# One raw bias table per near head, masked by GpSimd instead of VectorE, in a two-layer attention and expert kernel

## The reference, cut to what matters

```python
def one_row(r):
    r0 = jnp.clip(r - wr // 2, 0, rows - wr)             # rows = wr = 8: r0 is 0
    k_nb = ...[:, :, :, col_idx]                          # 16 columns around each query column
    bias = jnp.take(rpb_cols, r0 + jnp.arange(wr) - r + (NA_ROWS - 1), axis=1)
    s_loc = einsum(q_r, k_nb) * scale + transpose(bias)
    s_ctx = einsum(q_r, k_ctx) * scale
    p = softmax(concatenate([s_loc, s_ctx]))
```

## Time and profile before

| | us |
|---|---|
| median of 3 runs (3445.88 to 3447.69) | 3447.33 |
| the profiled execution | 3442.6 |
| its span in the profile | 3440.5 |
| end of the input projection, first mask load | 259.4 |
| first near scores | 327.4 |
| first product of the output projection | 487.9 |
| first U loads issued | 535.7 |

### The profile page before, as it was taken

The page is one execution under the profiler, slowest core; times in us unless marked ns, Lnnn a source line. Parts: engine busy times, 40 slices in busy tenths (PEclk is TensorE's granted clock), DMA queues, the critical chain, the costliest instruction groups (busy, mean ns, idle before and its releaser), DMA issues.

```text
span 3440.5 us, 45632 instructions
## 1 busy us (share of the span) xinstructions
PE 3297.2 (96%) x17004; PEld 2879.3 (84%) x17004; DVE 2183.3 (63%) x4167; ACT 1083.2 (31%) x1491; POOL 1837.6 (53%) x1166
## 2 busy tenths in 40 slices
PE   7998379999999999999999999999999999999999
PEld 3886257888878888999999778888888888999998
DVE  7877342488745422899998341688555323999997
ACT  3226244233334322222222333233334322222222
POOL 0000014347788861877772463357888752777761
PEclk9999689999999999999999999999999999999999
DMA  7772521146988894999998122255669865999995
GB/s 283 265 258 57 191 80 71 49 141 155 244 229 167 173 251 148 366 361 357 384 359 301 62 74 86 89 142 143 144 147 177 181 164 206 370 362 360 359 361 214
DMA packets 569952, 733.82 MB, mean 213 GB/s; under 512 B 272130, under 2 KB 404867, under 8 KB 553092
## 3 DMA queue, kind: packets, MB, share of 16 engines
q1 hardware_dynamic: 414084, 529.10, 47.5%
q0 software_dynamic: 118784, 134.68, 15.2%
q10 hardware_dynamic: 36864, 67.13, 5.4%
HBM read 610.92 MB, written 119.80 MB: 212 GB/s over the span
## 4 chain that ended last, share of the span: by engine, by line
PE 89%; SPq 5%; DVE 3%; DMA 1%; issue 1%; ACT 1%; DVEq 0%; ACTq 0%
PE ps L1508 41%; PE ps L1553 30%; PE ps L1468 5%; PE ps L1417 4%; PE ps L1280 4%; SPq L746 3%; SPq L728 1%; PE ps L1528 1%; PE ps L1458 1%; DVE macc L1793 1%; DMA modall<-in_w_mod 0%; DVE xm L1772 0%; PE ps L1232 0%; PE ps L1406 0%; SPq L739 0%
## 5 line engine op out<-in xcount | busy, mean ns | idle before, releaser
L1642 POOL DMA_INDIRECT G_scratch<-pick,gidx x512 | 887.0, 1732 | 283.1 <-issue 211.1
L1508 PE MATMUL ps<-xhi,Uhi 128*128 128x512 f32 x2048 | 801.0, 391 | 2.4 <-DVE Ulo L1992 2.4
L1508 PE MATMUL ps<-xhi,Ulo 128*128 128x512 f32 x2048 | 797.7, 390 | 0.0
L1508 PE MATMUL ps<-xlo,Uhi 128*128 128x512 f32 x2048 | 797.1, 389 | 0.0
L1553 PE MATMUL ps<-Hhi,Vhi 128*128 128x384 f32 x2048 | 686.0, 335 | 3.7 <-DVE Hlo L2202 3.7
L1553 PE MATMUL ps<-Hlo,Vhi 128*128 128x384 f32 x2048 | 684.7, 334 | 0.0
L1553 PE MATMUL ps<-Hhi,Vlo 128*128 128x384 f32 x2048 | 684.7, 334 | 0.0
L1992 DVE TENSOR_TENSOR Ulo<-Uraw,Uhi 128x1024 fp32r<-128x1024 f32 x230 | 281.8, 1226 | 578.9 <-ACT Uhi L1070 577.5
L1133 ACT CAST Vhi<-Vraw 128x1024 fp32r<-128x1024 f32 x256 | 269.9, 1054 | 779.6 <-PE ps L1553 764.6
L1649 POOL DMA_INDIRECT picked<-act_scratch,aidx x256 | 381.5, 1490 | 229.6 <-DMA act_scratch<-act_st 152.2
L1508 PEld LDWEIGHTS ps<-xhi,Uhi 128*128 128x128 f32 x2048 | 384.7, 188 | 81.3 <-DVE Ulo L1992 2.9
(11 more groups left out here) (297 smaller groups left out, 3979.2 us busy)
## 6 DMA issues: line engine op xcount, KB each, us to landing
Uraw<-in_UT SPq DMA_DIRECT2D x128, 1024.0 KB
Vraw<-in_V SPq DMA_DIRECT2D x256, 512.0 KB, 5.5
act_scratch<-act_st ACTq DMA_DIRECT2D x256, 256.0 KB
act<-act_scratch SPq DMA_DIRECT2D x256, 192.0 KB, 5.6
modw<-in_w_mod SPq DMA_DIRECT2D x80, 512.0 KB, 4.7
G_scratch<-zeros SPq DMA_DIRECT2D x32, 1024.0 KB, 10.2
Gin<-G_scratch SPq DMA_DIRECT2D x256, 128.0 KB
ring<-in_query SPq DMA_DIRECT2D x8, 2048.0 KB, 8.0
```

What stands on the lines that cost most here:

```text
L1508: mm = nc.tensor.matmul(up_bank(m), w, x[:, k, :], start=(k == 0 and j == 0), stop=(k == KT - 1 and j == 2))
L1642: nc.gpsimd.indirect_dma_start(G_dram[layer].rearrange("m p (t o) -> (m p t) o", o=1), bass.IndirectOffsetOnAxis(ap=gidx[r][:, h * TOPK + ...
```

## The change

There are five edits.

1. `braw` holds only the 8 to 40 band (256 elements a map). SyncE issues 16 loads a head, 64 in all. The three bands' tables are parts of this one, since the bias depends on the distance alone; `TABLE_PARTS` says which columns of it go where.
2. The mask comes in three DMAs, whose source is repeated over the 8 rows with a step of zero.
3. The 16 zero stores go out after the last query weight of the first four, ahead of the loads of U.
4. `masked_bias(h)` is GpSimd's, before `mix_rest`: wait for the loads; scale the raw table; for h of 2 and 3 wait until the exps of the last unit that reads the table buffer are done; ten additions. VectorE waits for `bias_masked` at the first maxima of each near head (`qt == 0`).
5. `xm` of n = 0: the reads are dense (`(r c) -> r c`) and the write goes through `(c r) -> r c`, with a step of 8 elements (32 bytes).

```diff
-TABLE_PARTS = (((0, 0, 24, 0), (1, 8, 32, 0)), ((1, 0, 8, 24), (2, 8, 24, 0), (2, 0, 8, 16)))
+TABLE_PARTS = (((0, 8, 32, 0), (1, 8, 32, 0)), ((1, 0, 8, 24), (2, 8, 24, 0), (2, 0, 8, 16)))
-        braw = [sb(f"braw{n}", at, [P, 2, TABLE_AT[-1]]) for n, at in enumerate((45, 168.5))]
+        braw = [sb(f"braw{n}", at, [P, 2, NEAR_W[1]]) for n, at in enumerate((45, 168.5))]
...
                     for n, j in enumerate(TABLE_BANDS):
-                        for r in range(NA_ROWS):
-                            sp.dma_start(mask[r:P:NA_ROWS, MASK_AT[n]:MASK_AT[n + 1]],
-                                         a["mask"][j * BAND:(j + 1) * BAND, BANDS[j][0]:BANDS[j][1]]
-                                         ).then_inc(bias_in[0], 16)
+                        c0, c1 = BANDS[j]
+                        sp.dma_start(mask[:, MASK_AT[n]:MASK_AT[n + 1]],
+                                     a["mask"][j * BAND:(j + 1) * BAND, c0:c1].unsqueeze(1).to_broadcast(
+                                         [BAND, NA_ROWS, c1 - c0])).then_inc(bias_in[0], 16)
                 for r in range(NA_ROWS):
-                    for n, j in enumerate(TABLE_BANDS):
-                        c0, c1 = BANDS[j]
-                        for m in range(2):
-                            sp.dma_start(
-                                braw[h % 2][r:P:NA_ROWS, m, TABLE_AT[n]:TABLE_AT[n + 1]].rearrange(
-                                    "q (s k) -> q s k", s=NA_ROWS),
-                                a["btab"][2 * h + m, j * BAND:(j + 1) * BAND,
-                                          NA_ROWS - 1 - r:2 * NA_ROWS - 1 - r, c0:c1]).then_inc(bias_in[h % 2], 16)
-                if h == 1:
-                    sp.wait_ge(zeros_ready, 1)
-                    for n in range(NZERO):
-                        zero_gates(0, n)
+                    for m in range(2):
+                        sp.dma_start(
+                            braw[h % 2][r:P:NA_ROWS, m, :].rearrange("q (s k) -> q s k", s=NA_ROWS),
+                            a["btab"][2 * h + m, BAND:2 * BAND, NA_ROWS - 1 - r:2 * NA_ROWS - 1 - r,
+                                      BANDS[1][0]:BANDS[1][1]]).then_inc(bias_in[h % 2], 16)
...
             load_chunk(W_Q0)
             load_chunk(W_Q0 + 1)
+            sp.wait_ge(zeros_ready, 1)
+            for n in range(NZERO):
+                zero_gates(0, n)
...
+            def masked_bias(h):
+                pool.wait_ge(bias_in[h % 2], 16 * (2 * NA_ROWS * (h // 2 + 1) + (0 if h % 2 else len(TABLE_BANDS))))
+                if h == 0:
+                    pool.wait_ge(proj_out, sum(e[0] == "copy" for e in in_evict) + 4)
+                    nc.gpsimd.tensor_scalar(mask[:, :], mask[:, :], 1.0 / QK_SCALE, None, ALU.mult)
+                nc.gpsimd.tensor_scalar(braw[h % 2][:, :, :], braw[h % 2][:, :, :], 1.0 / QK_SCALE, None, ALU.mult
+                                        ).then_inc(proj_out, 1)
+                pool.wait_ge(proj_out, sum(e[0] == "copy" for e in in_evict) + 5 + h)
+                if h >= 2:
+                    pool.wait_ge(exp_done, 2 * (HEAD_END + TT * (h - 1)))
+                for m in range(2):
+                    for n, c0, c1, to in TABLE_PARTS[0] + TABLE_PARTS[1]:
+                        rows = slice(TABLE_AT[n], TABLE_AT[n + 1])
+                        first = MASK_AT[n] + c0 - (8 if n == 0 else 0)
+                        last = nc.gpsimd.tensor_tensor(
+                            by_column(btab[h % 2][:, m, rows])[:, to:to + c1 - c0, :],
+                            by_row(braw[h % 2][:, m, :])[:, c0:c1, :],
+                            mask[:, first:first + c1 - c0].unsqueeze(2).to_broadcast([P, c1 - c0, NA_ROWS]), ALU.add)
+                last.then_inc(bias_masked, 1)
...
+            for h in range(HB // 2):
+                masked_bias(h)
             mix_rest(0, 2 * KT)
...
                     if n == 0:
-                        to, rows, roots_of = by_column(to), by_row(rows), by_row(inv)
+                        to = to.rearrange("p (c r) -> p r c", r=NA_ROWS)
+                        rows, roots_of = (x.rearrange("p (r c) -> p r c", r=NA_ROWS) for x in (rows, inv))
...
+                    if qt == 0:
+                        dve.wait_ge(bias_masked, h + 1)
...
                     maxima(u + 2)
-                    ahead = u + 2 + TT - HEAD_END
-                    if 0 <= ahead < TT * (HB // 2):
-                        masked_bias(ahead // TT, ahead % TT)
```

## The result

The changed kernel takes 3356.14 us (median of 4 runs, 3353.45 to 3358.24) beside 3446.61 for the kernel before (4 runs, 3445.07 to 3447.69): ratio 0.9737, 95% interval 0.9721 to 0.9754. It is faster by 90.5 us, and the forecast of 3362.4 (own range 3353 to 3371) was 6.3 too high. The sum was made against the profiled execution and is best judged there: forecast 3357.7, measured 3357.07, with a span of 3355.2 against 3440.5.

What follows compares the result with a forecast made beforehand. Bound in the near stretch: the number of DMA issues and one big transfer ahead of small ones, not bytes. 73.7 + 9.6 + 0.9 + 3.7 - 2.0 - 3.0 + 2.0 = 84.9 us off 3447.3 gives 3362.4, range 3353 to 3371.

Steps and rivals of the forecast that it cites:

- The stands: VectorE's three waits for table loads before making masked bias tables all go: 73.7 us gained.
- Masking off VectorE: Near units: twelve masking parts leave VectorE, each worth 0.8 of a 1.0 us difference between units: 9.6 us gained.
- GpSimd's sharing: VectorE operations beside GpSimd's new work lose time on the shared port pair, some 14 hits of 0.2 us: -3.0 us.
- Cold TensorE: Slow-clock transposes, products and scores behind the three stands go: 1.8 us a stand, two thirds counted, 3.7 us gained.
- the table change: ScalarE's function table change for the square root, formerly inside the 53 us stand, is uncovered before exps(20): -2.0 us.
- Diff units: Four masking parts in the last diff units leave VectorE, a quarter of them counted: 0.9 us gained.
- Zeros: The 16 zero stores, moved behind the second query weight on SyncE's queue, cost nothing; U loads keep 50 us to spare.
- Strided writes: Input scalings of xm: a strided write adds some 0.04 us, replacing strided reads; 2.0 us gained at the first projection product.
- rival 1: Strided writes of xm cost what strided reads do, so the input gives 0 to 1 us: 3364; chance 0.15.
- Rivals 2 and 3: Rival 2: only the stands go, masking and clock give nothing in the near units, 3373, chance 0.10. Rival 3: see its line.
- Rival 3: GpSimd's tables for heads 2 and 3 come late, from 17 us a head on; at 25 us, 3380; chance 0.09.
- Rival 4: Slower: GpSimd's tables far too late, break-even at 47 us a head, 3480 at 55; chance 0.02.

Runs made afterwards that it cites:

- e1: The changed kernel with the masking back on VectorE in its old 16 parts; 3364.65 us, ratio 0.9762.
- e5: The changed kernel with each head's ten GpSimd additions made twice; 3359.44 us, ratio 0.9754.
- e6: The changed kernel with each head's GpSimd additions made five times; 3377.21 us, ratio 0.9804.
- e4: The changed kernel with the scalings of xm dense on both sides, leaving out the reordering of the tokens; 3358.43 us in a single execution.
- e2: The changed kernel with the 16 zero stores back behind head 1's table loads, ahead of head 2's; 3359.24 us, ratio 0.9743.
- e11: The changed kernel itself run again, nothing changed; 3357.06 us, ratio 0.9744.
- e3: The kernel before with one edit, the zero stores moved behind the query weights; 3402.74 us, ratio 0.9875.
- e8: The changed kernel with the input scaling as before, two strided reads and a dense write; 3359.05 us, ratio 0.9753.
- e9: The changed kernel itself run again in more rounds, nothing changed; 3364.38 us, ratio 0.9725.

## Why the prediction was right, and where its terms were off

1. **The stands (73.7).** Right in full: no wait for `braw` is left, and the queue ends at 302.5, where the sum of its issues put it (305).
2. **Masking off VectorE (9.6) and GpSimd's sharing (-3.0).** Net 6.6 against 4.0 measured (e1 against after, clock aside). The step that failed is "0.8 x 12". Five columns gain 0.5 to 1.1 us, two 0.2, and two of the four with TensorE's spread products (L1372; columns 22 and 26, 4.26 with a part and 4.27 without) nothing. The row that would have told it stood in the earlier trace rows: the unit ending at 429.76 took 4.26 with a part and shows no wait, so TensorE was the limit there, and it was compared with 3.24, the turn to turn time of a unit without a spread. The sharing was too high as well: e5's second set of additions costs 1.0 us. If the first costs as much, which no run shows alone, the masking gave 5.0 where 9.6 were counted and the sharing took 1.0 where 3.0 were, and the smaller error hid part of the larger.
3. **Cold TensorE (3.7) and the table change (-2.0).** Net 1.7 against 4.8 measured. Before without its stands exceeds e1 without its dip: 1.9 to unit 17, 0.9 in 20, 0.9 in 24, 0.5 in 25, and 0.7 in the rest. The table change was counted at 2.0 and costs 1.31 (TensorE's wait in column 20; 1.06 in e1), so the clock was worth about 6 over three stands, by difference, a little past the upper bound of 5.5. "1.8 a stand" itself was right: e6, with two waits of a different cause, paid 1.9 and 1.8. Taking two thirds of it was the error.
4. **A clock term that wasn't on the list.** From the last turn the profiled execution of after reaches the output projection 1.4 us sooner than before and e1 to e4 do (5.59 for 7.02). That is luck of the execution, as e2 and e4 show, and no gain of the change. Points 2 to 4 give 4.0 + 4.8 + 1.4 = 10.2, and with 73.7 that is the 83.9 of the near units (forecast 82.0). The near sum came out because two errors of 2.6 and 3.1 us had opposite signs, which is luck too.
5. **Diff units (0.9).** Too high, and hidden: 69.01 us after against 67.98, with 66.1 to 69.0 over all profiles. Among profiles with the same clock at their start (0.83, last section) before has 67.98 and the changed kernels 67.49 to 67.73, so the parts were worth 0.25 to 0.5. The slower clock of after's profile cost it 1.3 us against e11's, about what the last column gave it.
6. **GpSimd.** 6.6 a head for 7. Ten additions are 5.1 us, where dense ones would be 4.3 by the earlier trace rows, so with reads that step 128 bytes they take about a fifth more. The Trainium skill (GPSIMD Engine Reference, Performance pitfalls for Q7 kernels) has half as much again for such reads, by which the ten would be some 6.4 us, an estimate. These additions don't show it, and the measurement decides.
7. **Zeros.** Cost nothing, as forecast, and bring nothing beside the smaller queue (e2). The forecast had counted their move as part of the cure and hadn't asked for its share; alone in the kernel before it is worth 43.9 us (e3).
8. **Strided writes (2.0).** The step "a strided write adds some 0.04" failed, and rival 1's mechanism held: 1122 ns, the very row 1125. A strided read beside a strided write adds nothing there (1125 for both, 1122 for the write alone), so that the difference of two such rows says nothing of either alone. The Trainium skill (SBUF - State Buffer, the "cachelines" note), which doesn't part reads from writes, was right here (748, 1122, 1346 ns). The result at the first product was 1.9 all the same (2.2 against e8), as 8 x (1.356 - 1.122) = 1.9 lies below the 2.3 us that TensorE's rows leave (51.14 to 48.83). Rival 1's time of 3364 was made with 0 to 1 for this and is refuted in that alone.
9. **The rest.** From the output projection on the forecast had nothing; the two rows of the table give -2.3 and +1.2. The median is 6.3 below the forecast mostly by the 4.7 us between before's profiled execution and its median, which were carried over: after's profiled execution lies 0.9 above its own median. On the spans, 84.9 us were forecast and 85.3 measured; the parts above missed by up to 3 us each.

Rivals 2 and 3 are out by the waits and by e1: masking and clock give 9 us (4.0 + 4.8) on top of the stands, and a head's table is ready 13 us early. Rival 3's place and about its threshold were shown by e6, which makes it come true (17 us forecast; the additions may take 18 to 19). Rival 4, slower, is far: with 26.5 us a head, four times what it is, e6 still leaves 68 of the 90 us. Its break-even of 47 wasn't tried.

## What to carry to other kernels

Count the DMA issues in front of a late load and multiply by the row of one: many small loads are bound by the queue that issues them, not by bytes, and here one raw table cut up by an idle engine was cheaper than three loaded ones. Compare a unit with a unit of the same kind when you price work taken off an engine, and look whether another engine ends it without a wait. A gap of 7 us in TensorE was paid twice here, the gap and about 1.8 us of cold products behind it (e6), and the place where an idle engine's new work lands beside the busy one is worth reading by itself (here the casts at unit 29).

## What the runs showed of the hardware

- **A strided write isn't free on VectorE.** 128x512 float32 with two inputs from SBUF: 748 ns dense, 1122 with the write stepping 32 bytes, 1346 to 1356 with two reads stepping 256 bytes.
- **TensorE's clock differs between executions of the same instructions.** Behind the gap at the end of the projection TensorE runs at the 1.2 GHz level for a while, and how long differs. The first 20 us from the first mask load in after, e11 and e9, three executions of one kernel:

```profile
258.05:278.05 20.00, 16.02 (x67) 9.82 (x66) 14.20 (x24) 10.09 (x22) 8.13 (x13) 0.74 0.46 128
```

```profile
256.44:276.44 20.00, 16.02 (x77) 9.99 (x77) 15.53 (x25) 11.26 (x26) 8.36 (x13) 0.83 0.46 128
```

```profile
256.47:276.47 20.00, 16.02 (x87) 10.31 (x87) 16.68 (x26) 11.79 (x26) 8.57 (x14) 0.91 0.46 128
```

  With granted clocks of 0.74, 0.83 and 0.91 their diff units take 69.01, 67.73 and 66.36 us, and the other eleven profiles fall in with one of the three: 68.8 to 69.0, 67.5 to 68.0, 66.1 to 66.6. The Trainium skill (TensorE: Matmul & The Clock Gate, The HAM clock gate) says that the number of cold products varies from run to run, and the traces agree. So terms under 2 us are not to be read from one pair of profiles, unless they are read turn by turn or at an equal clock.
- **The same wait drops the clock once and once not.** In e1 TensorE waited 1.62 us for `Abuf` twice. Behind the first, at 356.87, came seven us at 0.53; behind the second, at 369.37, the transposes took 1.09 us as ever.
- **GpSimd beside VectorE.** The pair of 448-element scalings takes 0.82 us alone and 2.40 beside GpSimd's subtractions of 512 elements (1.28 each), in before and after alike; beside GpSimd's additions of 0.5 us one of 768 elements takes 1144 and 1156 ns in after, where it takes 1017 to 1020 without them.
